# Dilated attention on 384 keys per query, in whole float32, in a two-layer hybrid encoder

## What is computed

```python
DIL_PATTERNS = ((128, 1), (512, 4), (2048, 16))
offsets = [d * np.arange(-((w // 2) // d), (w // 2) // d + 1) for (w, d) in DIL_PATTERNS]
for off in offsets:
    idx = pos[:, None] + off[None, :]
    s = jnp.where(valid, jnp.einsum(q_blk, k_sel) * scale, NEG_INF)
    lse = jax.nn.logsumexp(s, axis=-1, keepdims=True)
    outs.append(einsum(exp(s - lse), v_sel)); lses.append(lse)
out = sum(softmax(lses) * outs)
```

## Time and profile before

| | |
|---|---|
| Median of 3 executions | 525.67 us (525.66 to 526.03) |
| Span of the profiled execution | 523.6 us |
| Busy: TensorE / VectorE / ScalarE / GpSimd | 513.4 / 379.6 / 269.8 / 164.3 us |
| Fast products of the projections (L612 to L614) | 3 x 480 of 512 columns |
| Score products L722 | 240 records |
| Transposes L735 | 192 records |
| Dilated value products L759, local L768 | 192 and 256 records |
| Loads of v | 40 issues: 24 of 64 KB, 16 of 112 KB |
| DMA engines busy, from HBM | 96.51 MB moved, mean 184 GB/s |

### The profile page before, as it was taken

The page is one execution under the profiler, slowest core; times in us unless marked ns, Lnnn a source line. Parts: engine busy times, 40 slices in busy tenths (PEclk is TensorE's granted clock), DMA queues, the critical chain, the costliest instruction groups (busy, mean ns, idle before and its releaser), DMA issues.

```text
span 523.6 us, 7833 instructions
## 1 busy us (share of the span) xinstructions
PE 513.4 (98%) x2782; PEld 400.7 (77%) x2782; DVE 379.6 (73%) x753; ACT 269.8 (52%) x503; POOL 164.3 (31%) x224
## 2 busy tenths in 40 slices
PE   8999999999999999999999999999999999999995
PEld 7888777587686888778888887876768768878884
DVE  6879797989994766621539969988999667852424
ACT  6713367656666475434423216756666565652214
POOL 0114232222123466425411224122121345673101
PEclk9999999999999999999999999999999999999999
DMA  8725688668676897999503468975985969999973
GB/s 280 282 76 137 156 194 223 158 172 187 167 174 166 207 254 160 246 227 287 158 2 100 111 131 187 231 169 137 210 181 132 233 141 264 226 229 233 210 175 160
DMA packets 44261, 96.51 MB, mean 184 GB/s; under 512 B 7488, under 2 KB 21312, under 8 KB 44224
## 3 DMA queue, kind: packets, MB, share of 16 engines
q0 software_dynamic: 19648, 62.93, 53.4%
q1 hardware_dynamic: 24288, 32.91, 20.5%
q10 hardware_dynamic: 288, 0.19, 0.2%
HBM read 81.84 MB, written 4.72 MB: 165 GB/s over the span
## 4 chain that ended last, share of the span: by engine, by line
PE 82%; DMA 8%; DVE 4%; issue 2%; POOL 1%; SPq 1%; ACT 1%; POOLq 0%; DVEq 0%; ACTq 0%
PE acc L612 18%; PE acc L614 17%; PE acc L613 17%; PE sc L722 4%; PE misc L759 4%; DMA sq<-sq 4%; PE tp L735 4%; DMA w_lo<-w_out 3%; PE sc L674 1%; PE sc L675 1%; PE sc L676 1%; SPq L502 1%; PE sc L612 1%; PE sc L614 1%; PE sc L613 1%
## 5 line engine op out<-in xcount | busy, mean ns | idle before, releaser
L612 PE MATMUL acc<-act_hi,w_hi 128*128 128x512 f32 x480 | 194.5, 405 | 0.7 <-DMA w_lo<-w_out 0.7
L614 PE MATMUL acc<-act_lo,w_hi 128*128 128x512 f32 x480 | 187.5, 391 | 0.0
L613 PE MATMUL acc<-act_hi,w_lo 128*128 128x512 f32 x480 | 187.5, 391 | 0.0
L612 PEld LDWEIGHTS acc<-act_hi,w_hi 128*128 128x128 f32 x480 | 90.2, 188 | 22.7 <-issue 3.1
L614 PEld LDWEIGHTS acc<-act_lo,w_hi 128*128 128x128 f32 x480 | 90.1, 188 | 19.9
L613 PEld LDWEIGHTS acc<-act_hi,w_lo 128*128 128x128 f32 x480 | 90.4, 188 | 17.4 <-issue 0.5
L852 ACT ACTIVATE w_lo<-w_hi 128x1024 fp32r<-128x1024 f32 (+1 forms) x62 | 61.9, 999 | 48.0 <-DMA w_hi<-w_out 36.2
L914 ACT ACTIVATE prob<-prob,nmx 128x512 f32<-128x512 f32 (+1 forms) x80 | 50.4, 629 | 40.4 <-DVE nmx L1307 40.4
L1067 POOL DMA_DIRECT2D w_lo<-w_in x40 | 36.1, 903 | 102.4 <-ACT w_lo L852 101.6
L1285 DVE SCALAR_TENSOR_TENSOR y<-ub,par,y 128x512 f32<-128x512 f32 x90 | 68.2, 758 | 0.0
L1285 DVE SCALAR_TENSOR_TENSOR ub<-ub,par 128x512 f32<-128x512 f32 x84 | 64.8, 771 | 0.0
(11 more groups left out here) (152 smaller groups left out, 763.5 us busy)
## 6 DMA issues: line engine op xcount, KB each, us to landing
w_hi<-w_in POOLq DMA_DIRECT2D x40, 512.0 KB, 5.9
w_lo<-w_in POOLq DMA_DIRECT2D x40, 512.0 KB, 6.3
w_hi<-w_out POOLq DMA_DIRECT2D x16, 512.0 KB, 6.4
w_lo<-w_out POOLq DMA_DIRECT2D x16, 512.0 KB, 7.5
pT<-w_in SPq DMA_DIRECT2D x15, 512.0 KB, 5.1
sq<-sq SPq DMA_DIRECT2D x48, 64.0 KB, 2.5
gf<-nabias SPq DMA_DIRECT2D x20, 128.0 KB, 5.4
v_way<-vs SPq DMA_DIRECT2D x8, 256.0 KB, 3.1
```

Of the source, the lines that this page charges most:

```text
L612: nc.tensor.matmul(to[:, :], w_hi[:, slot, k, :], a_hi[:, k, :], start=i == 0, stop=False)
L613: nc.tensor.matmul(to[:, :], w_lo[:, slot, k, :], a_hi[:, k, :], start=False, stop=False)
L614: last = nc.tensor.matmul(to[:, :], w_hi[:, slot, k, :], a_lo[:, k, :], start=False, stop=i == K - 1)
```

## The change

A query block now scores 384 key columns: 256 near ones (a window of 256 tokens around the block, `NEAR_LO`) and 128 of its own class modulo four. To make the class a slice, queries, keys and values of the dilated heads are stored by class: within each block of 128 for queries and the near windows, over the whole sequence for keys. The table `cnt` becomes four blocks of 384 columns, in which a far column within 64 of the query is masked, and a near one beyond 64. Queries and keys, local ones too, stay in whole float32: the hi and lo copies, `qk_split`, `split_lo` and their semaphores go. Softmax steps and transposes work on 384 columns. `v` gets four more blocks of 32 (the far keys), and a dilated pair's values are loaded in 28 DMAs. The slots of stores and loads (`V_STORES`, `V_LOADS`) stay.

```diff
-        q_hi = sb("q_hi", [P, 2, SEQ], F32R)
...
+        queries = sb("q", [P, 2, SEQ])
+        keys = sb("k", [P, 2, SEQ])
+        v = sb("v", [P, 2, 4, (NA_BLOCKS + CLASSES) * BLK])
...
+        def v_moves(g):
+            return (3 + QUADS) * QUADS if g < DPAIRS else QUADS
...
                 for j in range(QUADS):
                     to = v[BLK * j:BLK * (j + 1), g % 2]
                     if g < DPAIRS:
-                        to, t = to[:, :, 0:BLK * QT], quadrant(v_way[l, g], j)
+                        half = BLK // 2
+                        low = NEAR_ODD.stop - NEAR_ODD.start
+                        t = v_way[l, g].rearrange("(i p) (j c) -> j p i c", p=BLK, j=QUADS)
+                        sp.dma_start(to[:, :, NEAR_EVEN], t[j]).then_inc(v_moved[g % 2], 16)
+                        sp.dma_start(to[0:half, :, NEAR_ODD], t[j][half:BLK, :, 0:low]).then_inc(v_moved[g % 2], 16)
+                        sp.dma_start(to[half:BLK, :, NEAR_ODD], t[j][0:half, :, BLK:BLK + low])\
+                            .then_inc(v_moved[g % 2], 16)
+                        t = v_way[l, g].rearrange("(i p) (r j c) -> j i p r c", p=BLK, r=CLASSES, j=QUADS)[j]
+                        for i in range(QUADS):
+                            sp.dma_start(to[:, i, FAR].rearrange("p (r c) -> p r c", r=CLASSES), t[i])\
+                                .then_inc(v_moved[g % 2], 16)
...
                 for b in range(b, b + 2):
-                    first, w = (0, SEQ) if g < DPAIRS else (ROWS * NA_LO[b], NKEY)
-                    for i, (q, k) in enumerate(((q_hi, k_hi), (q_lo, k_hi), (q_hi, k_lo))):
...
+                    for h in range(2):
+                        own = slice(HD * h, HD * (h + 1))
+                        t = keys[own, g % 2, :]
+                        if g < DPAIRS:
+                            t = t.rearrange("p (r a) -> p r a", r=CLASSES)[:, :, NEAR_LO[b]:NEAR_LO[b] + 2 * PCLS]
+                            t, w = t.rearrange("p r (u a) -> p u r a", u=2), NEAR
+                        else:
+                            t, w = t[:, ROWS * NA_LO[b]:ROWS * NA_LO[b] + NKEY], NKEY
+                        last = nc.tensor.matmul(sc[2 * (b % 2) + h][:, 0:w], queries[own, g % 2, b * P:(b + 1) * P], t,
+                                                start=True, stop=True)
...
+                if g < DPAIRS:
+                    for b in range(b - 1, b + 1):
+                        for r in range(CLASSES):
+                            for h in range(2):
+                                own, rows = slice(HD * h, HD * (h + 1)), slice(PCLS * r, PCLS * (r + 1))
+                                last = nc.tensor.matmul(sc[2 * (b % 2) + h][rows, NEAR:DKEY],
+                                                        queries[own, g % 2, b * P + PCLS * r:b * P + PCLS * (r + 1)],
+                                                        keys[own, g % 2, P * r:P * (r + 1)], start=True, stop=True)
...
-                for k in range(QT):
-                    last = nc.tensor.transpose(tp[:, k * P:(k + 1) * P],
+                for i in range(DKEY // P):
+                    last = nc.tensor.transpose(tp[:, i * P:(i + 1) * P],
...
-                pe.wait_ge(v_moved[g % 2], MOVED * v_uses(l, g))
+                pe.wait_ge(v_moved[g % 2], v_landed(l, g))
...
+                    for r in range(CLASSES):
                         for i in range(QUADS):
...
+                            nc.tensor.matmul(of_class(ob[BLK * i:BLK * (i + 1), :], r), v_of(g, i, far_block(r)),
+                                             of_class(pT[:, BLK * i // HD, 2, :], r), start=r == 0, stop=False)
+                    for b in range(QT):
+                        for half in range(2):
+                            for i in range(QUADS):
+                                last = nc.tensor.matmul(ob[BLK * i:BLK * (i + 1), b * P:(b + 1) * P],
...
-                nc.vector.tensor_tensor(z, z, zsw, ALU.add).then_inc(zc_ready, 1)
...
+                if r % 2:
+                    to = by_class(keys[:, r // 2 % 2, :])
+                    ins = nc.vector.tensor_tensor(to, in_order(z), in_order(zsw), ALU.add)
+                else:
...
+                    to = queries[:, r // 2 % 2, :].rearrange("p (b r a) -> p b a r", b=QT, r=CLASSES)
+                    ins = nc.vector.tensor_tensor(to, by_block(z), by_block(zsw), ALU.add)
+                ins.then_inc(qk_ready, 1)
```

More of the change, by code:

```diff
@@ L89 @@
 NA_BLOCKS = (SEQ - P) // NA_STEP + 1
-NEG_TILE = 896
+PCLS = P // CLASSES
+NEAR = 2 * P
+DKEY = NEAR + P
+NEAR_LO = [min(max(P * b - REACH, 0), SEQ - NEAR) // CLASSES for b in range(QT)]
+assert BLK == PCLS and all(d == 1 or d % CLASSES == 0 for _, d in PATTERNS)
 BIASES, BIAS_RING, BIAS_AT = UNITS - DUNITS, 6, 14
@@ L403, in build, with v_landed @@
         QUADS = P // BLK
-        MOVED = 16 * QUADS
+        NEAR_EVEN, NEAR_ODD = slice(0, QT * BLK), slice(QT * BLK, NA_BLOCKS * BLK)
+        FAR = slice(NA_BLOCKS * BLK, (NA_BLOCKS + CLASSES) * BLK)
+        def v_moves(g):
+            return (3 + QUADS) * QUADS if g < DPAIRS else QUADS
+        def v_landed(l, g):
+            pairs = [(m, p) for m in range(l + 1) for p in range(PAIRS) if p % 2 == g % 2 and (m, p) <= (l, g)]
+            return sum(16 * v_moves(p) for _, p in pairs)
         V_STORES = {4: 0, 12: 1, 16: 2, 23: 3, 31: 4}
@@ L717, in scores @@
                 for b in range(b, b + 2):
-                    first, w = (0, SEQ) if g < DPAIRS else (ROWS * NA_LO[b], NKEY)
-                    for i, (q, k) in enumerate(((q_hi, k_hi), (q_lo, k_hi), (q_hi, k_lo))):
[L720 to L725, removed]
+                    for h in range(2):
[8 more added lines that the diff above has]
+                                                start=True, stop=True)
+                        if g >= DPAIRS:
+                            last.then_inc(s_ready, 1)
+                if g < DPAIRS:
+                    for b in range(b - 1, b + 1):
[5 more added lines that the diff above has]
+                                                        keys[own, g % 2, P * r:P * (r + 1)], start=True, stop=True)
+                                if r == CLASSES - 1:
+                                    last.then_inc(s_ready, 1)
             def turn(l, n):
@@ L1212, in empty_tile @@
                     is_k = kind == "bk"
[L1213 to L1214 removed]
+                    if j or l:
+                        dve.wait_ge(qk_ready, ROPES * l + 2 * j - 1 + is_k)
                     nc.vector.tensor_tensor(zc[:, int(is_k), :], zs, cs[:, 0, :], ALU.mult).then_inc(dve_own, 1)
@@ L1301, in maxima @@
                 if g < DPAIRS:
-                    w, add = SEQ, cnt[:, P * (QT - 1 - b):P * (QT - 1 - b) + SEQ]
+                    w, add = DKEY, cnt[:, DKEY * b:DKEY * (b + 1)]
                 else:
@@ L1436, in _ @@
                 for c in range(PRE):
-                    if (gk := HI_AT.get(2 * (c - PRE))) is not None:
-                        split_lo(l, *gk)
                     if taps_first(c):
@@ L1480, in _ @@
                         empty_tile(l, c)
-                    if (gk := HI_AT.get(n - 1)) is not None:
-                        split_lo(l, *gk)
                     if n == 0 or n % 2 or not taps_first(tile_at(n - 1)[0]):
@@ L1571, in dil_table @@
 def dil_table():
-    diff = np.arange(NEG_TILE)[None, :] - P * (QT - 1) - np.arange(P)[:, None]
-    count = np.zeros(diff.shape, np.int64)
-    for w, d in PATTERNS:
-        count += (np.abs(diff) <= (w // 2) // d * d) & (diff % d == 0)
-    return np.where(count > 0, np.log(np.maximum(count, 1)), NEG).astype(np.float32)
+    r, a = np.meshgrid(np.arange(CLASSES), np.arange(PCLS), indexing="ij")
+    r, a = r.ravel(), a.ravel()
+    tables = []
+    for b in range(QT):
+        query = CLASSES * (PCLS * b + a) + r
+        near = [CLASSES * (NEAR_LO[b] + PCLS * half + a) + r for half in range(2)]
+        key = np.broadcast_to(np.concatenate(near), (P, NEAR))
+        key = np.concatenate([key, CLASSES * np.arange(P)[None, :] + r[:, None]], 1)
+        diff = key - query[:, None]
+        count = np.zeros(diff.shape, np.int64)
+        for w, d in PATTERNS:
+            count += (np.abs(diff) <= (w // 2) // d * d) & (diff % d == 0)
+        count *= (np.abs(diff) <= REACH) == (np.arange(DKEY) < NEAR)[None, :]
+        tables.append(np.where(count > 0, np.log(np.maximum(count, 1)), NEG))
+    return np.concatenate(tables, 1).astype(np.float32)
 def rope_table():
```

91 lines of the change are left out of this document (38 added, 53 removed).

## The result

The changed kernel takes 555.17 us in the median of 4 runs (554.33 to 559.07), the kernel before 525.66 us: a ratio of 1.0572, 95% interval 1.0543 to 1.0602. It is slower by 29.5 us, where the prediction had 13; 555.17 lies just above its range. The profiled execution took 554.33 us, with a span of 552.7 against 523.6 before: 29.1 us to account for. Intervals leave out executions over 1.5% above the fastest of the same kernel, one each of few_dmas and kept_again.

The account below looks back on a forecast made before the run. The prediction took TensorE's list of instructions as the bound. It summed 525.7 - 10 (TensorE's own work) + 20 (waits for values) + 3 (clock) = 538.7 and said 538.5 us, range 524 to 555 us.

Parts of the forecast that it names:

- Direction and mechanism: Forecast that trains of 28 value loads make TensorE wait at pairs 0 and 1, not pair 2; slower; chance 0.70.
- pair 0's waits: TensorE's wait before pair 0's value products: 7.2 us in layer 0, 6.5 us in layer 1.
- The train, T = 19.0 us: A dilated pair's 28 value loads on SP's queue: 15.7 us from first to last issue, 3.3 us for landing.
- Pair 1, 5 and 1.5 us: TensorE's waits before pair 1's value products: 5 us in layer 0, 1.5 us in layer 1.
- The clock, +3 us: TensorE's clock falls to half speed behind the two waits longer than 4.8 us, costing 1.5 us each.
- TensorE's own -10 us: TensorE's instruction list without waits: -5.3 - 4.9 + 0 + 0.7 = -9.5 us, and about -0.5 for small holes.
- Transposes: Four to three in each of 48 units on TensorE, 0.11 us each: -5.3 us.
- value products: Six dilated pairs' products on TensorE, 2.75 us each in place of 3.57: -4.9 us.
- Scores: TensorE's score blocks: dilated 1.54 us, taken as no change over 12 blocks; local 0.99 for 0.90, +0.7 us over 8.
- rival C: New tiles overlap less: far tiles four at a time, 544 us; float32 heads one after the other, 556; chance 0.11.
- B: Value loads come in time and TensorE's saving shows: 516 to 522 us; chance 0.14.
- D: Trains slower than average because weights share the DMA engines: T = 26, waits of 48 us, 566 us; chance 0.05.

Follow-up runs that it names:

- few_dmas: The changed kernel with values stored in DRAM as one 128-channel row per key, keys by class: 4 stores and 9 loads per dilated pair; 523.41 us, 0.9938.
- kept_again: The changed kernel with idle float32 products ahead of the wait for values in pairs 0 and 1, keeping TensorE's clock up; 554.82 us, 1.054.
- far_once: The changed kernel with one far load per quadrant in whole 512 B rows, 16 issues for 28, far values wrong; 530.34 us, 1.0083.
- before_28: The kernel before with each dilated pair's four value loads cut into 28, nothing else of the change; 540.32 us, 1.0266.
- far_rows: The changed kernel, still 28 issues, far loads in 512-byte pieces for 128, same bytes, far values wrong; 549.61 us, 1.044.

## Why the prediction was wrong, by its steps

**Direction and mechanism: right.** TensorE waits for v at pairs 0 and 1 in both layers and not at pair 2; far_once, before_28 and few_dmas show that the loads on SP's list are the cause. The sizes were wrong: 16 us of profiled time in four terms, pair 0's waits 5.0, pair 1's 4.0, the clock 3.7 and TensorE's own work 3.2. All four had one sign, and any one of them set right would have put the time inside the range.

**The train, T = 19.0 us: the step that failed.** It ran from the first issue to the value products in 21.3, 19.0, 22.3 and 19.2 us. The 0.58 us for an issue, the mean of four short trains with 512-byte pieces, became 0.61 to 0.69. The far issue, with 128-byte pieces, was priced at nothing extra: 599 ns against 423 in far_rows, where T is 19.3 and 20.2 for pair 0. Counted from start to start, as the prediction did, pair 0's 27 issues took 18.1 and 18.5 us for 15.7 and the landing 3.2 and 3.8 for 3.3. For pair 1 T came out by luck: 16.6 and 17.1 us of issues, with landings of 2.5 and 2.2. The ground given for counting issues and not their size, a store of 256 KB in 0.34 us, was misread: that store is issued after SP has waited, when a load takes 0.31 us too; right behind another DMA the store takes 0.43 (at 144.31 in the changed kernel) and not 0.58. The room, from the first issue to the moment at which TensorE asks, was 12.6 and 12.4 us for 11.8 and 12.5, though in layer 1 both ends lie some 14 us later than before. So the wait of pair 0 became 21.32 - 12.56 = 8.8 us and 22.3 - 12.4 = 9.9, for 7.2 and 6.5: +5.0, of which the trains gave 5.6 and the room took 0.7 back.

**Pair 1, 5 and 1.5 us.** Layer 0's 5 was 5.2. Layer 1's 1.5 was 5.3, since the room was read off one execution in which the store had landed in 2.4 us; after the change it took 5.7 and 5.6 in the two layers, and the room from load to products was 13.9 in both, for 12.6 and 16.8. A distance that holds a transfer's landing isn't fixed: +3.8 us. It doesn't look like chance either: 5.3 to 5.4 us in far_once and far_rows in layer 0, but 2.0 in both layers of before_28. What sets it isn't shown. Together the waits are 29.2 for 20.

**The clock, +3 us.** The fall behind pair 0's waits was foreseen at 1.5 each and cost 1.8 and 1.9 us. Pair 1's waits of 5 us also brought one, 1.4 and 1.5 us that stood in no sum: 6.7 in all, 3.7 over. The fall had been placed 4.8 us after the last matmul, as at the program's end; in pair 0 of layer 0 the mean of 0.71 over 95.00 to 106.28 puts it near 99.7, some 2 us after the last product's end, and far_once has a fall in a wait of 3.9 us. kept_again shows that this is no sum to be had back alone.

**TensorE's own -10 us: -6.8.** Transposes (0.11 us each) and value products (2.76 for 2.75) came out to a hundredth. Scores cost +2.1 for +0.7: a local block took 1.06 for 0.99, a dilated one 1.66 for 1.54. The eight far tiles do overlap in full, which had been the large doubt (rival C, 5 to 18 us): 32 matmuls of 64x128, four passes of eight, ran from 58.57 to 59.17. What was missed is the price of a new shape at a block's start: its first pass took 0.32 us where the others took 0.22, and the step to the far tiles 0.31. The Trainium skill (TensorEngine Tiling (Array Packing), Key Properties) says that a change of mode drains the array; the step inside the dilated block shows 0.1 us of it, as the sum had taken, and half of the 0.2 that the rule was priced at; the other miss is the same 0.1 at each block's start. The small holes, taken at -0.5, grew by about 1.3.

**Rivals.** B (in time, 516 to 522) needed trains under 16 us; it describes few_dmas, not the change. D gave the right sign on the trains: slower than their average, though not for the reason named alone, as before_28 with its weights in flight ran at 0.48 to 0.54. The small pieces are the larger part: 2.0 us of each T of pair 0. The argument against D, that weight loads stop while TensorE waits, held in part only: the weights' share of the DMA engines was 77% before the first wait, 51% over 97.6 to 103.7 and still 44% from there to the wait's end. On small pieces the Trainium skill (DMA: Bandwidth & Descriptors, opening table) gives 512 B as the least transfer for full rate. For 128 bytes the runs agree, as far as the issue goes: 599 against 423 ns for equal bytes, and 5 us of the kernel's time. For 256 bytes the issue shows nothing of it: before_28's loads, six of seven in such pieces, take 423 ns too. The rule was told in the prediction and given no weight in the sum; T = 21 to 22 would have followed from a price of 0.18 us for each of 16 far issues, and 4 x 2.9 = 12 us more of waits at most, an estimate.

**Range.** Its upper end let T go to 23 and kept the other terms at their likely values. The misses of four terms had one sign, and two of them a common cause (longer waits bring more and longer falls of the clock), which a range made from single terms doesn't hold.

## What to carry to other kernels

Where an engine's list has slack for four small DMA issues, it need not have it for 28: count the issues, price each at what the same queue shows for pieces of that size, and add a transfer's landing as it is on a bad day (7 to 8 us in far_once, for 3.3 that were planned). If data must be gathered in a new pattern, lay them out in DRAM so that the gather is a few DMAs with long pieces; here that turned +5.7% into -0.6% with the same arithmetic. Don't cure a late load by moving it up a shared list before seeing who waits for what it is moved past.

## What the runs showed that was not expected

- The time in SP's queue of one issue depends on the pieces and on what stands before it, and little on the bytes: 16 KB as 128-byte pieces 599 ns, as 512-byte pieces 423, 64 KB as 512-byte pieces 432 (far_once); the first issue after a wait of SP 0.31 to 0.34 us, for 64 KB and for 256 KB.
- Four stores in 128-byte pieces (few_dmas) took 3.8 to 8.9 us to land, median 5.8, and, with a swap ahead that took 1.2 us longer, held its first load until 89.55, 4.6 us later than in the changed kernel. No value product waited for it, since nine loads need 5 us; 0.6 us were left.
- Eight float32 tiles of 64 rows by 32 columns of outputs run fully side by side: the passes of eight start 0.109 us apart, as those of four do for the value products.
- Idle products kept the granted clock at full speed through waits of 9 us, and the kernel's median changed by under 1 us. In the one trace 2.9 of 6.7 us are lost to later landings; why they are later, and what takes the rest in other executions, stays open.
